# Down-projection of a hybrid block: block products, seven for eight, in two passes, with weight differences from adding transfers

## The chip, the cores and the metric

One Trainium2 chip, one core. The metric is the device time of one launch in microseconds, the median of three runs. Five engines work side by side, each with its own queue: TensorE (PE), VectorE (DVE), ScalarE (ACT), GpSimd (POOL) and SyncE (SP, which here only issues transfers).

## What is computed

One layer of a two-branch block for 640 tokens (512 latent tokens and 128 context tokens, D_MODEL = 1024, D_FF = 2816), in f32. The change touches its last stage, the down-projection of the gated ConvFFN and the residual behind it:

```python
def conv_ffn(h, w_up, w_conv, b_conv, w_down):
    u = h @ w_up                       # 640 x 1024 by 1024 x 5632
    u = conv_general_dilated(u, ...) + b_conv     # depthwise, width 3
    a, g = jnp.split(u, 2, axis=-1)
    return (a * jax.nn.silu(g)) @ w_down          # 640 x 2816 by 2816 x 1024

h2 = rmsnorm(x, g_ffn) * (1 + sc2) + sh2
x = x + gt2 * conv_ffn(h2, w_up, w_conv, b_conv, w_down)
```

## The kernel before

**Products in f32.** Every f32 operand is split into a high part (fp32r, written by ScalarE) and a low part (value less high part, a subtraction on GpSimd or VectorE). A product is three matmuls: high by high, high by low, low by high.

**Up-projection.** The 2816 gate channels are 22 tiles (NF) of 128, the first two plain, the other 20 by block products: 7 products P1 to P7 for 8, each of 4 k-tiles by 320 columns, 84 matmuls a tile. The loop over cycles c stands in each engine's program. GpSimd makes the weight sums S1 and S3 (`pooled`) and the low parts of six weight blocks (`unit_low`, L880). ScalarE makes the high parts (`unit_high`, L2199), takes P1 out (`taken`), and does the middle tap of the convolution (`first_tap`, L2172) and the SiLU (`gate_silu`, L2179). VectorE adds the products (L2976, L2983), does the outer taps (`conv_ahead` L2901, `conv_behind` L2908), the sums S2 and S4, and `gate_product` (L2922), which leaves the activations of tile j in `prod[:, j, :]`, 128 channels by 640 tokens.

**Down-projection.** w_down comes in 22 chunks: column half c (512 columns), two rows of 128 channels each. SyncE loads a chunk as two transfers of 256 KB into `wraw` (L640, two slots), ScalarE writes the high part `whi` (L2220, waits until TensorE has done with the slot), GpSimd the low part `wlo` (L713). TensorE (`token_major`, L1533 to L1535) runs, per chunk, 5 token tiles by 2 rows by 3 matmuls of 512 columns. The high parts of the activations are ScalarE's (`act_high_part`, L2227), the low parts VectorE's (`act_low_part`, L3002). The first chunk has buffers of its own (`first_raw`, `first_hi`, `first_lo`), so that it starts beside the last cycle of the up-projection. A token tile is finished by `residual` on VectorE (L2814: product by gate row; L2817: added to x), and its store is issued by ScalarE. The five stores of the first column half go out in mid-stage.

```python
for n in range(N_DOWN):
    c, q = n // 11, n % 11
    pe.wait_ge(lo_done, L_DOWN + n + 1)
    ...
    for t in range(NT) if n else (4, 0, 1, 2, 3):
        for k in range(2):
            mm = token_major(DOWN_BANK[t, c], a_hi, a_lo, 0, t, w_hi[:, k, :], w_lo[:, k, :], ...)
```

The order of all this is written out by hand: each engine runs its own list, and counters (semaphores) say what may start.

## Time and profile before

| | |
|---|---|
| median of 3 runs | 970.99 us (970.53 to 971.38) |
| span of the profiled execution | 968.6 us |
| its own time | not given apart from the span; the median is 2.4 us above the span |
| TensorE, VectorE, ScalarE, GpSimd busy | 98%, 62%, 45%, 52% |
| TensorE clock granted | full in all 40 slices |
| HBM read, written | 101.45 MB, 4.47 MB |

The span runs from the first to the last instruction of the program; a run's time holds the launch around it as well. The down-projection is the last 150 us of the span, the up-projection by block products the 240 us before it. "Busy" for TensorE is the time with a matmul in flight, and several are in flight at once: the pace, start to start, is the number to read. "Idle before, releaser" names the engine whose work ended a wait.

### The profile page before, as it was taken

To read this page: it belongs to the slowest core of one execution; us is meant where nothing else is said; L and a number is where in the kernel's file an instruction comes from. 1 tells how busy PE (TensorE), PEld (TensorE's weight loads), DVE (VectorE), ACT (ScalarE), POOL (GpSimd) and SP (SyncE) were. 2 spreads that over 40 slices of the span, in tenths; PEclk is the share of its full clock that TensorE was granted. 3 is DMA by queue.
4 is the path that set the end of the run, shared out by engine and by line. 5 is a ranking of instruction groups with operands and counts; after the bars stand their busy time and mean duration, and the time that the engine had idled before them with its cause. 6 is when DMAs were issued, how large, how long until landed. Compare 5 with 4: busy or idle time off the path is not lost.

```text
span 968.6 us, 18808 instructions
## 1 busy us (share of the span) xinstructions
PE 952.3 (98%) x7513; PEld 866.9 (89%) x7513; DVE 603.2 (62%) x1087; ACT 434.7 (45%) x683; POOL 503.9 (52%) x361
## 2 busy tenths in 40 slices
PE   6999999999999999999999999999999999999998
PEld 5799899977888899999987999999999999888886
DVE  6508359963575769434937998777777778903002
ACT  5244165523766564342404465555555556511110
POOL 1386723323332317772724378888888885433331
PEclk9999999999999999999999999999999999999999
DMA  9896222126011133888641313222222222322331
GB/s 335 270 157 97 78 76 55 58 77 185 23 30 38 45 86 100 265 251 296 236 152 44 88 45 87 88 86 84 82 83 82 83 83 72 121 81 82 105 107 55
DMA packets 127826, 108.20 MB, mean 112 GB/s; under 512 B 8342, under 2 KB 104571, under 8 KB 127483
## 3 DMA queue, kind: packets, MB, share of 16 engines
q1 hardware_dynamic: 122728, 99.81, 34.1%
q0 software_dynamic: 1696, 3.25, 2.3%
q10 hardware_dynamic: 3315, 3.94, 1.1%
q8 instruction: 60, 0.98, 0.4%
q14 instruction: 27, 0.22, 0.1%
HBM read 101.45 MB, written 4.47 MB: 109 GB/s over the span
## 4 chain that ended last, share of the span: by engine, by line
PE 87%; DVE 5%; SPq 2%; issue 2%; POOL 1%; ACT 1%; DMA 1%; DVEq 0%; POOLq 0%; ACTq 0%
PE PA L1649 6%; PE PA L1647 6%; PE PA L1648 6%; PE PJ L923 6%; PE PJ L928 5%; PE PJ L924 5%; PE PA L1533 3%; PE PA L1535 3%; PE PA L1534 3%; PE PJ L1533 3%; PE PJ L1535 3%; PE PJ L1534 3%; PE PJ L1441 2%; PE PA L1367 2%; PE PJ L1442 2%
## 5 line engine op out<-in xcount | busy, mean ns | idle before, releaser
L713 POOL TENSOR_TENSOR wlo<-wraw,whi 128x1024 fp32r<-128x1024 f32 x53 | 133.1, 2513 | 257.4 <-ACT whi L1704 167.4
L923 PE MATMUL PJ<-h_hi,whi 128*128 128x320 f32 x336 | 104.8, 320 | 0.1
L924 PE MATMUL PJ<-h_lo,whi 128*128 128x320 f32 x336 | 101.1, 309 | 0.0
L928 PE MATMUL PJ<-h_hi,wlo 128*128 128x320 f32 x336 | 76.5, 309 | 0.0
L1704 ACT ACTIVATE whi<-wraw 128x1024 fp32r<-128x1024 f32 x39 | 41.0, 1052 | 71.8 <-PE PJ L928 23.2
L923 PEld LDWEIGHTS PJ<-h_hi,whi 128*128 128x128 f32 x336 | 63.0, 188 | 5.8 <-issue 3.6
L2220 ACT ACTIVATE whi<-wraw 128x1024 fp32r<-128x1024 f32 x21 | 22.3, 1060 | 98.6 <-PE PA L1535 51.6
L924 PEld LDWEIGHTS PJ<-h_lo,whi 128*128 128x128 f32 x336 | 63.1, 188 | 0.0
L880 POOL TENSOR_TENSOR behind<-behind_val,behind 128x512 fp32r<-128x512 f32 x40 | 52.0, 1301 | 19.0 <-ACT behind L2199 19.0
L1649 PE MATMUL PA<-h_hi,behind 128*128 128x320 f32 x192 | 59.3, 309 | 0.0
L928 PEld LDWEIGHTS PJ<-h_hi,wlo 128*128 128x128 f32 x336 | 56.1, 188 | 0.0
L2901 DVE SCALAR_TENSOR_TENSOR PJ<-u_all,vec,PJ 128x641 f32<-128x641 f32 x44 | 39.0, 887 | 18.6 <-ACT PJ L2172 18.6
L1535 PE MATMUL PA<-whi,prod_lo 128*128 128x512 f32 x124 | 48.3, 389 | 0.0
L771 POOL TENSOR_TENSOR wlo<-wraw,whi 128x256 fp32r<-128x256 f32 x24 | 17.0, 737 | 57.7 <-ACT whi L1704 57.7
L2814 DVE TENSOR_TENSOR down_diag<-PJ,g_rows 128x512 f32<-128x512 f32 x4 | 2.8, 690 | 65.3 <-PE PJ L1535 65.3
L2172 ACT ACTIVATE PJ<-u_all,vec 128x641 f32<-128x641 f32 x44 | 38.9, 884 | 5.6 <-DVE prod L2923 3.4
L2199 ACT ACTIVATE behind<-behind_val 128x512 fp32r<-128x512 f32 x40 | 25.0, 625 | 34.8 <-POOL behind_val L891 34.4
L1647 PE MATMUL PA<-h_hi,behind 128*128 128x320 f32 x128 | 39.6, 310 | 0.5 <-issue 0.5
L2908 DVE SCALAR_TENSOR_TENSOR PJ<-u_all,vec,PJ 128x641 f32<-128x641 f32 x44 | 39.2, 890 | 1.5
L1647 PE MATMUL PA<-h_hi,ahead 128*128 128x320 f32 x128 | 39.7, 310 | 0.2 <-DVE u_all L2984 0.2
L1648 PE MATMUL PA<-h_lo,behind 128*128 128x320 f32 x128 | 39.6, 309 | 0.0
L1647 PE MATMUL PA<-T_hi,ahead 128*128 128x320 f32 x128 | 39.6, 309 | 0.0
(593 smaller groups left out, 3234.3 us busy)
## 6 DMA issues: line engine op xcount, KB each, us to landing
wraw<-in_w_in_dram SPq DMA_DIRECT2D x72, 256.0 KB, 3.2
ada_rest<-in_w_ada_dram SPq DMA_DIRECT2D x32, 512.0 KB, 6.1
wraw<-in_w_up_dram SPq DMA_DIRECT2D x48, 256.0 KB, 3.8
wraw<-in_w_down_dram SPq DMA_DIRECT2D x42, 256.0 KB, 3.0
raw_even<-in_w_up_dram SPq DMA_DIRECT2D x40, 256.0 KB, 3.6
ada<-in_w_ada_dram SPq DMA_DIRECT2D x16, 512.0 KB, 7.5
out_dram<-x ACTq DMA_DIRECT2D x10, 256.0 KB, 2.1
x_rows<-in_x_sample_dram SPq DMA_DIRECT2D x2, 1024.0 KB, 6.5
```

What stands on the lines that cost most here:

```text
L713: pool.tensor_tensor(wlo[:, slot, 0:k, :], wraw[:, slot, 0:k, :], whi[:, slot, 0:k, :].bitcast(F32), ALU.subtract).then_inc(lo_done, done)
L880: pool.tensor_tensor(unit_lo[name], value_of(j, name), unit_hi[name].bitcast(F32), ALU.subtract).then_inc(lo_done, 1)
L923: pe.matmul(out, whi[:, slot, w0 + k, :], hi(k)[:, tok], start=start and k == k0, stop=False)
L924: pe.matmul(out, whi[:, slot, w0 + k, :], lo(k)[:, tok], start=False, stop=False)
L928: mm = pe.matmul(out, wlo[:, slot, w0 + k, :], hi(k)[:, tok], start=False, stop=stop and k == k1 - 1)
L1533: pe.matmul(psum(*bank), act_hi_[:, k, tok], w_hi, start=start, stop=False)
L1534: pe.matmul(psum(*bank), act_hi_[:, k, tok], w_lo, start=False, stop=False)
L1535: return pe.matmul(psum(*bank), act_lo_[:, k, tok], w_hi, start=False, stop=stop)
L1647: pe.matmul(out, w_hi[:, k, :], b_hi[:, k, :], start=k == 0, stop=False)
L1648: pe.matmul(out, w_hi[:, k, :], b_lo[:, k, :], start=False, stop=False)
L1649: mm = pe.matmul(out, w_lo[:, k, :], b_hi[:, k, :], start=False, stop=k == 3)
L1704: act.activation(whi[:, slot, :, :], wraw[:, slot, :, :], ACT.Copy).then_inc(hi_done, done)
```

## The change

The 512 latent tokens' part of the down-projection is done by block products. Its operands are halved three ways: tokens (near 0 to 255, far 256 to 511), the 22 tiles of channels (k and k + 11, KH = 11), the output columns (0 to 511 and 512 to 1023). Seven products stand for eight; each is 2 token tiles by 11 steps by 3 matmuls of 512 columns. The 128 context tokens ("C") stay plain.

- **First pass**, 11 steps: P1, P2, P3 and the context tokens, 30 matmuls a step. Raw rows k and k + 11 are loaded whole (two transfers of 512 KB, `down_rows`, into `d_raw`, two slots). P3 needs a difference of activations, which VectorE forms (`third`, `second_fourth`, `first_of`).
- **Second pass**, 11 steps: P5, P7, P6, P4, 24 matmuls a step, with differences of weights. Two of the four weight blocks of a step are formed ahead, in the up-projection: SyncE loads a row (512 KB), ScalarE writes it negated (`ahead_negative`), GpSimd issues a transfer that adds other rows to it out of HBM (`accum_op`), and SyncE stores it in `ahead_dram`; eleven times, in cycles 4 to 14. The other two are made on VectorE (`weight_sums`).
- **Low parts**: half of them by transfers. ScalarE writes the high part negated, and a transfer from GpSimd's queue adds the raw value out of HBM (`landing_low`). The others are VectorE's (`weight_low`, `far_low_units`). GpSimd makes none in this stage.
- **Three sets** of high and low weights (`W_SETS`), the last three steps of the second pass run product by product (`N_LAST`), products are taken out by ScalarE between the passes (`taken_out`), GpSimd and VectorE share the final sums, and SyncE issues all stores.
- The convolution of the last channel tile goes through SBUF (`conv_of`) and stands later in the queues, since the PSUM banks go to P1.

The diff, cut to what the text speaks of:

```diff
+                q = j - FIRST_AHEAD - 2
+                if 0 <= q < KH:
+                    sp.wait_ge(ahead_sum[q % 2], AHEAD_SUM[q % 2] + 16 * (q // 2 + 1))
+                    sp.dma_start(ahead_dram[q], d_ahead[q % 3][:, :, :]).then_inc(ahead_stored[q % 3], 16)
+                q = j - FIRST_AHEAD
+                if 0 <= q < KH:
+                    if q == 0:
+                        sp.wait_ge(h2lo_set, 2 * NK + 4)
+                    elif q >= 3:
+                        sp.wait_ge(ahead_stored[q % 3], AHEAD_STORE + 16 * (q // 3))
+                    sp.dma_start(d_ahead[q % 3][:, :, :], w_dn_v[:, q, :].rearrange("p (c n) -> p c n", c=2)).then_inc(ahead_in[q % 3], 16)
...
+            def down_rows(n):
+                if n == 0:
+                    sp.wait_ge(lo_done, C_WIN + LOWS["A12", NF - 2])
+                elif n == 1:
+                    sp.wait_ge(up_ps, BLOCKS + 2 * N_PLAIN + PRODUCTS["P4", NF - 1])
+                elif n - 2 < KH:
+                    sp.wait_ge(hi_done, H_DOWN + 3 * (n - 2) + 2)
+                    sp.wait_ge(actlo_set, PART_LOW["weight", n - 2])
+                else:
+                    sp.wait_ge(actlo_set, PART_LOW["far", n - 2 - KH])
...
+                for h in range(2):
+                    rows = w_dn_v[:, n % KH + KH * h, :].rearrange("p (c n) -> p c n", c=2) if h or n < KH else ahead_dram[n - KH]
+                    sp.dma_start(d_raw[n % 2][:, 2 * h:2 * h + 2, :], rows).then_inc(raw_in[n % 2 ^ 1], 16)
...
+                q = c - FIRST_AHEAD
+                if 0 <= q < KH:
+                    pool.wait_ge(ahead_neg, 1 + q + 1)
+                    pool.dma_start(d_ahead[q % 3][:, :, :], ahead_rows(q), accum_op=ALU.add).then_inc(ahead_sum[q % 2], 16)
                 unit_low(c, "A12")
...
+            def landing_low(n):
+                k = n % KH
+                if n < KH:
+                    pool.wait_ge(hi_done, H_DOWN + 3 * n + 3)
+                    out, rows = d_far[n % W_SETS][:, :, :], w_dn_v[:, k + KH, :].rearrange("p (c n) -> p c n", c=2)
+                else:
+                    pool.wait_ge(hi_done, H_DOWN + 3 * n + 2)
+                    out, rows = d_low(n, 1), ahead_dram[k, :, 1, :]
+                pool.dma_start(out, rows, accum_op=ALU.add).then_inc(low_landed[n % W_SETS], 16)
+            for n in range(KH):
+                landing_low(n)
...
+            for n in range(KH):
+                slot, last = n % W_SETS, n == KH - 1
+                t_hi, t_lo = c_hi[slot][:, 0, :], c_lo[slot][:, 0, :]
+                s_hi4, s_lo4 = c_hi[slot][:, 1, :], c_lo[slot][:, 1, :]
+                pe.wait_ge(actlo_set, PART_LOW["rows", n])
+                if n == 0:
+                    pe.wait_ge(prod_set, NF - 1)
+                for i in range(2):
+                    mm = down(d_bank("P1", i), tile_of(a_hi[slot][:, 0, :], i), tile_of(a_lo[slot][:, 0, :], i), n, 0, n == 0, last)
+                if last:
+                    mm.then_inc(dn_done, 1)
+                pe.wait_ge(actlo_set, PART_LOW["last", n])
+                if n == 0:
+                    pe.wait_ge(add_set, ADDED["U2", NF - 1])
+                for c in range(2):
+                    mm = down(d_bank("C", c), tile_of(t_hi, 0), tile_of(t_lo, 0), n, c, n == 0, False)
+                mm.then_inc(dn_ps, 1)
+                pe.wait_ge(low_landed[n % W_SETS], landed_low(n))
+                if n == 0:
+                    pe.wait_ge(add_set, ADDED["C21", NF - 1])
+                for i in range(2):
+                    mm = down(d_bank("P2", i), tile_of(a_hi[slot][:, 1, :], i), tile_of(a_lo[slot][:, 1, :], i), n, 2, n == 0, last)
+                if last:
+                    mm.then_inc(dn_done, 1)
+                mm = down(d_bank("C", 0), tile_of(t_hi, 1), tile_of(t_lo, 1), n, 2, False, last)
+                if last:
+                    mm.then_inc(dn_done, 1)
+                pe.wait_ge(actlo_set, PART_LOW["fourth", n])
+                if n == 0:
+                    pe.wait_ge(add_set, ADDED["C11", NF - 1])
+                for i in range(2):
+                    mm = down(d_bank("P3", i), tile_of(s_hi4, i), tile_of(s_lo4, i), n, 3, n == 0, last)
+                if last:
+                    mm.then_inc(dn_done, 1)
+                mm = down(d_bank("C", 1), tile_of(t_hi, 1), tile_of(t_lo, 1), n, 3, False, last)
+                mm.then_inc(dn_ps, 1)
...
+            for k in range(KH - N_LAST):
+                for p, name in enumerate(("P5", "P7", "P6", "P4")):
+                    sum_ready(name, k)
+                    if k == 0:
+                        pe.wait_ge(ev_set, E_DOWN + {"P5": 2, "P7": 4, "P6": 7, "P4": 8}[name])
+                    for i in range(2):
+                        mm = sum_product(name, k, i)
+                    if p % 2:
+                        mm.then_inc(dn_ps, 1)
+            for name in D_LAST:
+                for i in range(2):
+                    for k in range(KH - N_LAST, KH):
+                        if i == 0:
+                            sum_ready(name, k)
+                        mm = sum_product(name, k, i)
+                    mm.then_inc(dn_done, 1)
...
+            def down_high(n, h):
+                units = slice(2 * h, 2 * h + 2)
+                if n < KH or h == 0:
+                    act.wait_ge(raw_in[n % 2 ^ 1], raw_down(n))
+                else:
+                    act.wait_ge(sum_set, T_DOWN + 2 * (n - KH) + 2)
+                if n == 0:
+                    product_done("P5", NF - 1)
+                elif n == 1:
+                    product_done("P7", NF - 1)
+                elif n == 2:
+                    product_done("P2", NF - 1)
+                else:
+                    act.wait_ge(dn_ps, 2 * (n - W_SETS) + h + 1)
+                act.activation(d_hi[n % W_SETS][:, units, :], d_raw[n % 2][:, units, :], ACT.Copy).then_inc(hi_done, 1)
+            def down_negative(n):
+                out, units = (d_far[n % W_SETS][:, :, :], slice(2, 4)) if n < KH else (d_near[n % W_SETS][:, 1:2, :], slice(1, 2))
+                act.wait_ge(hi_done, H_DOWN + 3 * n + (2 if n < KH else 1))
+                if KH <= n < KH + W_SETS:
+                    act.wait_ge(dn_ps, 2 * (n - W_SETS) + 2)
+                act.activation(out, d_hi[n % W_SETS][:, units, :].bitcast(F32), ACT.Copy, scale=-1.0).then_inc(hi_done, 1)
+            def first_half(n):
+                down_high(n, 0)
+                down_negative(n)
...
+                if m == NF - 1:
+                    act.wait_ge(lo_done, L_DOWN)
+                    down_negative(0)
+                    down_high(1, 0)
+                    fourth_high(0)
+                    down_high(1, 1)
+                    down_negative(1)
+                    early_high(0)
+                    down_rows_high(1)
+                    fourth_high(1)
+                    early_high(1)
...
+            def weight_sums(k):
+                n = KH + k
+                raw = d_raw[n % 2]
+                dve.wait_ge(raw_in[n % 2 ^ 1], raw_down(n))
+                dve.tensor_tensor(raw[:, 3, :], raw[:, 3, :], raw[:, 0, :], ALU.subtract).then_inc(sum_set, 1)
+                dve.wait_ge(sum_set, T_DOWN + 2 * k + 1)
+                dve.tensor_tensor(raw[:, 2, :], raw[:, 2, :], raw[:, 3, :], ALU.subtract).then_inc(sum_set, 1)
...
+                if c == NF - 1:
+                    third(0)
+                    weight_low(0)
+                    rows_low(0)
+                near_sum("C21", c, "P4", ug[:, near], ug[:, near])
+                if c == NF - 1:
+                    last_low(0)
+                far_sum("C12", c, "P3", tmp[:, :], ua[:, c % 2, :])
                 fourth_sum(c + 1)
                 if c == NF - 1:
-                    act_low_part(2)
-                elif c < NF:
-                    last_sum(c)
+                    second_fourth(0)
+                last_sum(c)
+                if c < NF - 1:
                     conv(c, 1)
-            for k in range(4, 10):
-                act_low_part(k)
-            for k in range(10, NF):
-                act_low_part(k)
+            fourth_low(0)
+            first_of(0)
+            third(1)
+            second_fourth(1)
+            weight_low(1)
+            rows_low(1)
+            last_low(1)
+            first_of(1)
+            fourth_low(1)
+            early_low(0)
+            conv(NF - 1, 1)
+            conv(NF - 1, 0)
+            gate_product(NF - 1)
+            for k in range(2, KH):
+                third(k)
+                early_low(k - 1)
+                second_fourth(k)
+                weight_low(k)
+                rows_low(k)
+                last_low(k)
+                first_of(k)
+                fourth_low(k)
+            early_low(KH - 1)
+            weight_sums(0)
+            weight_low(KH)
+            sums_low(0)
+            weight_sums(1)
+            far_low_units(0)
...
+            for k in range(1, KH):
+                weight_low(KH + k)
+                sums_low(k)
+                if 2 <= k < 6:
+                    context_out((k - 2) // 2, k % 2)
+                if k + 1 < KH:
+                    weight_sums(k + 1)
+                far_low_units(k)
```

Where instructions stand now, in three places. First GpSimd, in one cycle of the up-projection (cycle 5; the L numbers of the changed kernel are its own). `behind_val` is S3 or S4, `s_val` S1. Before:

```order
L880 TENSOR_TENSOR behind<-behind_val,behind 128x512
L880 TENSOR_TENSOR behind<-wraw,ahead 128x512
L880 TENSOR_TENSOR ahead<-raw_even,ahead 128x512
L891 TENSOR_TENSOR s_val<-raw_even 128x512
L880 TENSOR_TENSOR ahead<-s_val,ahead 128x512
```

With the change:

```order
L989 TENSOR_TENSOR behind<-behind_val,behind 128x512
L1006 DMA d_ahead_204<-in_w_down_dram 128x2x512
L989 TENSOR_TENSOR behind<-wraw,ahead 128x512
L989 TENSOR_TENSOR ahead<-raw_even,ahead 128x512
L1000 TENSOR_TENSOR s_val<-raw_even 128x512
L989 TENSOR_TENSOR ahead<-s_val,ahead 128x512
```

One adding transfer stands between the low part of S4 and that of A12, in eleven cycles; everything else keeps its place.

VectorE behind the last product of the convolution; before it has the low parts of the activations and the final sums:

```order
L2923 TENSOR_TENSOR prod<-PJ,cg 128x128
L3002 TENSOR_TENSOR prod_lo<-prod,act_mid 128x640 x11
L3002 TENSOR_TENSOR prod_lo<-prod,act_late 128x640 x7
L2814 TENSOR_TENSOR down_diag<-PA,g_rows 128x512
```

With the change, in the second pass, steps 0 to 2 (L3347, L3349: `weight_sums`; L3357: `weight_low`; L3340: `sums_low`; L3364: `far_low_units`; d_raw_206 and 207 are the two slots):

```order
L3347 TENSOR_TENSOR d_raw_206<-d_raw_206 128x512
L3349 TENSOR_TENSOR d_raw_206<-d_raw_206 128x512
L3364 TENSOR_TENSOR d_far_202<-d_raw_207,d_hi_196 128x1024
L3357 TENSOR_TENSOR d_near_197<-d_raw_206,d_hi_194 128x512
L3340 TENSOR_TENSOR prod_lo<-prod,s_hi_224 128x2x256
L3347 TENSOR_TENSOR d_raw_207<-d_raw_207 128x512
L3349 TENSOR_TENSOR d_raw_207<-d_raw_207 128x512
L3364 TENSOR_TENSOR d_far_200<-d_raw_206,d_hi_194 128x1024
L3357 TENSOR_TENSOR d_near_198<-d_raw_207,d_hi_195 128x512
```

Each `far_low_units` of one slot stands behind the two `weight_sums` of the other slot.

SyncE, the loads of w_down; before two slots of half chunks:

```order
L698 DMA first_raw_194<-in_w_down_dram 128x512
L640 DMA wraw<-in_w_down_dram 128x512 x8
L652 DMA g_rows<-gate_dram 128x2048
L640 DMA wraw<-in_w_down_dram 128x512 x34
```

With the change, across the border of the passes:

```order
L788 DMA d_raw_206<-in_w_down_dram 128x1024 x2
L788 DMA d_raw_207<-ahead_dram 128x1024
L788 DMA d_raw_207<-in_w_down_dram 128x1024
L788 DMA d_raw_206<-ahead_dram 128x1024
L788 DMA d_raw_206<-in_w_down_dram 128x1024
```

A load is now twice 512 KB, and in the second pass half of it comes from `ahead_dram`.

## Rows read from the trace of the kernel before

**Rows 1.** The page: span, TensorE's busy time, GB/s in 40 slices.
```profile
span 968.6 us, 18808 instructions
...
PE 952.3 (98%) x7513; PEld 866.9 (89%) x7513; DVE 603.2 (62%) x1087; ACT 434.7 (45%) x683; POOL 503.9 (52%) x361
...
GB/s 335 270 157 97 78 76 55 58 77 185 23 30 38 45 86 100 265 251 296 236 152 44 88 45 87 88 86 84 82 83 82 83 83 72 121 81 82 105 107 55
```

**Rows 2.** Timeline, ScalarE: start us, us, engine, line, operation [idle before <-releaser].
```profile
849.13 1.06 ACT L2220 ACTIVATE whi<-wraw 128x1024 fp32r<-128x1024 f32 x1 [4.48 <-PE PJ L1535]
855.93 1.06 ACT L2220 ACTIVATE whi<-wraw 128x1024 fp32r<-128x1024 f32 x1 [5.74 <-PE PJ L1535]
```

**Rows 3.** Windows: us, busy PE, PEld, DVE, ACT, POOL; clock, DMA share, GB/s.
```profile
815.00:965.00 150.00, 149.45 (x658) 123.06 (x657) 43.72 (x49) 35.29 (x41) 51.38 (x21) 1.00 0.26 88
```

**Rows 4.** Windows, the same columns, in the up-projection.
```profile
700.00:800.00 100.00, 100.00 (x684) 100.00 (x683) 77.68 (x147) 53.87 (x89) 83.97 (x65) 1.00 0.30 87
```

**Rows 5.** Timeline, GpSimd, cycles of the up-projection.
```profile
600.45 1.30 POOL L880 TENSOR_TENSOR ahead<-wraw,ahead 128x512 fp32r<-128x512 f32 x1 [0.37 <-ACT ahead L2199]
...
612.58 1.29 POOL L880 TENSOR_TENSOR ahead<-raw_even,ahead 128x512 fp32r<-128x512 f32 x1 [0.37 <-ACT ahead L2199]
...
711.00 1.29 POOL L880 TENSOR_TENSOR ahead<-raw_even,ahead 128x512 fp32r<-128x512 f32 x1 [0.38 <-ACT ahead L2199]
...
760.27 1.30 POOL L880 TENSOR_TENSOR ahead<-raw_even,ahead 128x512 fp32r<-128x512 f32 x1 [0.37 <-ACT ahead L2199]
...
800.58 1.48 POOL L880 TENSOR_TENSOR ahead<-s_val,ahead 128x512 fp32r<-128x512 f32 x1 [0.80 <-ACT ahead L2199]
```

**Rows 6.** Timeline, ScalarE, the SiLU of one cycle.
```profile
807.23 0.71 ACT L2179 ACTIVATE cg<-PJ 128x641 f32<-128x641 f32 x1 [0.48 <-DVE PJ L2908]
```

**Rows 7.** Transfers of GpSimd: issues (timeline), then KB and us to landing (page).
```profile
40.97 0.95 POOL L719 DMA_DIRECT2D kc_tok<-in_cache_na_k_dram  x1 [22.82 <-PE PA L972]
...
46.15 0.77 POOL L724 DMA_DIRECT2D vc<-in_cache_na_v_dram  x1
...
q0 software_dynamic: 1696, 3.25, 2.3%
...
kc_tok<-in_cache_na_k_dram POOLq DMA_DIRECT2D x1, 512.0 KB, 3.9
vc<-in_cache_na_v_dram POOLq DMA_DIRECT2D x1, 512.0 KB, 4.4
```

**Rows 8.** Timeline, TensorE: first matmul of the last P5; border to the down-projection.
```profile
803.69 0.31 PE L1647 MATMUL PA<-T_hi,ahead 128*128 128x320 f32 x1
...
814.10 0.31 PE L1649 MATMUL PA<-h_hi,behind 128*128 128x320 f32 x1
814.28 0.47 PE L1533 MATMUL PJ<-first_hi,act_early 128*128 128x512 f32 x1
```

**Rows 9.** Timeline, VectorE: conv_ahead of channel tile 20, and the last residual.
```profile
810.82 0.88 DVE L2901 SCALAR_TENSOR_TENSOR PJ<-u_all,vec,PJ 128x641 f32<-128x641 f32 x1
...
964.73 0.69 DVE L2814 TENSOR_TENSOR down_diag<-PA,g_rows 128x512 f32<-128x512 f32 x1
965.46 0.69 DVE L2817 TENSOR_TENSOR x<-x,down_diag 128x512 f32<-128x512 f32 x1
```

**Rows 10.** One line's instructions, L3002: duration ns min/median/max.
```profile
L3002 DVE TENSOR_TENSOR prod_lo<-prod,act_mid x12: 811/813/3031, 817.5 to 836.3; 128x640 fp32r<-128x640 f32 x12
```

**Rows 11.** A load pair of w_down: issue (timeline), landing of all 50 (L640), window.
```profile
859.49 0.80 SPq L640 DMA_DIRECT2D wraw<-in_w_down_dram  x2
...
DMA to landing us min/median/max: 2.6/3.1/7.5
...
862.00:863.00 1.00, 1.00 (x7) 0.81 (x6) 0.00 (x0) 0.27 (x1) 0.00 (x0) 1.00 0.27 102
```

**Rows 12.** DMA issues, window 815 to 965: the load of the gate rows.
```profile
g_rows<-gate_dram SPq DMA_DIRECT2D x1, 1024.0 KB, 7.6
```

**Rows 13.** Windows, the first 10 us.
```profile
0.00:10.00 10.00, 3.22 (x16) 3.25 (x17) 6.84 (x12) 3.32 (x4) 0.19 (x4) 1.00 0.80 283
```

457 lines of the change are left out of this document (319 added, 138 removed).

## Prediction, made before the changed kernel ran

> **What bounds the kernel now.** I read the page first: TensorE is busy 98% of the span [rows 1]. A busy share says little of the pace, so I took the stretch of the down-projection: one of its 22 weight chunks follows the other every 6.80 us (849.13 to 855.93), and what ScalarE waits for there is TensorE [rows 2]. A chunk has 30 matmuls, so a matmul of 512 columns takes 0.2267 us, and 660 of them 149.6 us. The stretch from 815 to 965 has 149.45 us of them [rows 3]: TensorE is the bound and has no pause. In the up-projection before it TensorE is full too, but GpSimd is 84% busy and ScalarE 54% [rows 4]. Granted clock: 1.00 in every stretch, the higher of the two levels.
>
> **Matmuls removed.** First pass, 11 steps of 30 matmuls, second pass, 11 steps of 24: 594 for 660, all of 512 columns. 66 x 0.2267 = **-15.0 us** if TensorE stays fed. The rest asks whether it does.
>
> **Up-projection, extra work in a loop that is nearly full.** Four cycles of GpSimd take 49.27 us (711.00 to 760.27), 12.32 each, and so do 84 matmuls. Early, before the cycles fall into TensorE's step, one took 12.13 (600.45 to 612.58) [rows 5]. So the round GpSimd, ScalarE, VectorE, ScalarE, GpSimd has 0.19 us to spare per cycle. Its waits, 0.37 and 0.80 of GpSimd and 0.48 of ScalarE, are for each other, none for TensorE [rows 5, 6]. The change puts one 1024-wide negation on ScalarE (1.06, of which 0.97 is pace) ahead of the SiLU, which waits 0.48 there now [rows 6], so +0.49; and one transfer issue on GpSimd (0.77 to 0.95 [rows 7], I take 0.85) ahead of a 0.36 wait, so +0.49 too, at the same time. A cycle is then 12.62 for 12.32: 11 cycles x 0.30 = 3.3 us late. P5's low part is ready at 800.58 + 1.48 = 802.06 and its matmuls start at 803.69 [rows 5, 8]: 1.6 us of reserve. **+1.7 us**. Ends: 0 (if the issue overlaps) and +6 (if an adding issue takes 1.3 us).
>
> **Start of the down-projection.** The first down matmul now starts at 814.28, at once behind the last of the up-projection [rows 8]. In the change VectorE must, from the end of conv_ahead at 811.74 (start 810.82, pace 0.92), do conv_behind, gate_product, third(0), weight_low(0) of 1024 elements and rows_low(0) of 512. By the 0.69 for 512 elements and 0.81 for 640 [rows 9, 10], 256 take about 0.42 and 1024 about 1.2; the chain ends at 815.7, **+1.5 us**. P2, the third matmul group of step 0, then wants the low part that is landed by an adding transfer. The negation for it stands on ScalarE behind first_tap(21), which waits for C21, now at 815.9 on VectorE behind those low parts; it ends at 818.0, and GpSimd issues then. Plain GpSimd transfers of 512 KB land in 3.9 and 4.4 us [rows 7]; beside 2 MB of loads (the next rows, and g_rows, which took 7.6 [rows 12]) I take 5. TensorE is free for it at 818.5: **+4.6 us**, ends +3.5 and +8. Behind that, the last channel's convolution on VectorE and ScalarE (four steps of 0.9 and a SiLU, each waiting for the other) holds VectorE until 831.0, so that rows_low(2) comes at 834.6 for 834.0: **+0.7 us**.
>
> **First pass, steady.** Per step of 6.80 us VectorE has 6 ops of 256 (0.34 each in a row), 2 of 512 and one of 1024, 4.3 us, ScalarE three of 1024, two of 512 and two of 256, about 4.6: fed, and gaining over a us a step. 1.5 MB per step over 6.8 us is 230 GB/s, under the 335 that the first slices move [rows 1]. **0**.
>
> **Second pass, the term that decides.** VectorE's order in a step k is weight_low, sums_low, weight_sums(k+1), far_low_units(k). weight_sums(k+1) needs the rows of step k+1, and SyncE issues those only when far_low_units(k-1) has freed their buffer. So far(k-1), load, weight_sums(k+1), far(k) is one closed chain: the two buffers don't overlap, since far(k) stands behind a wait for the other one's load. Its period:
> - the load. Now, SyncE issues two transfers of 256 KB from 859.49 on, and their bytes flow into the stretch 862 to 863 [rows 11]. The second is issued 0.4 later and lands 3.1 after that [rows 11], so 3.5 for 0.5 MB. The change loads 1 MB: 0.5 MB more at 335 GB/s is 1.6, so 5.1. The adding transfer of the step before, 256 KB, falls right beside it: +0.8. **5.9 us**;
> - weight_sums: 0.73 (a dependent step, 964.73 to 965.46) and 0.62 (0.69 less the overlap with what follows) [rows 9], far_low_units 1.2, and 0.05 of signalling: **2.6 us**.
>
> Together 8.5 us per step, where 24 matmuls take 5.44. Let T be the end of the first pass. sums_high(0) waits until TensorE has finished step 9 (T-6.8), so far(0) ends at T-2.8; far(1) follows at T+6.0, since sums_high(1) stands behind the last eviction. P6(2) would start at T+13.6 and far(2) comes at T+14.5: from step 2 on the chain leads. far(9) comes at T+6.0+8x8.5 = T+74.0, far(10) at T+76.4, and 66 matmuls (15.0 us) stand behind it: T+91.5. Unhindered, 264 matmuls take 59.9. **+31.6 us**.
> Ends of the load: below 4.6 (3.1 us of bytes and some 1.5 around them) without the neighbour, above 7.6 (the 1 MB of g_rows in this stretch, [rows 12]): 8 x 1.3 = 10 us less, 8 x 1.7 = 14 more.
> The Trainium skill, "DMA: Bandwidth & Descriptors", section "Anatomy of one DMA", fits a transfer issued by GpSimd as 2.0 us plus bytes over 436 GB/s. For 1 MB that would be 4.4, a chain of 7.0 and a sum 12 us below mine; the row (3.1 where the fit says 2.6 for 256 KB) speaks against the fit here, and the time still stays far above before.
>
> **Tail.** Now two VectorE steps follow the last product (964.73, 965.46), and the span ends 2.5 us behind the second [rows 1, 9]. The change ends with the same two; GpSimd's last adds fall about 1 us before the end, and may meet them: **+0.3**.
>
> **Sum.** 968.6 - 15.0 + 1.7 + 1.5 + 4.6 + 0.7 + 31.6 + 0.3 = 994.0 us of span. The runs' median, 970.99, is 2.4 above the profiled span (the profiled execution's own time isn't given apart), so **996 us** against 970.99. A measurement of this kernel tells apart about 0.2%, 2 us.
>
> **Rivals.**
> 1. *The chain doesn't bind.* If the loads of the second pass run ahead in a way that I misread, 31.6 falls to the 1.1 us of the last step's buffer wait: 965.9, faster. Against it: the period must be under 5.44, so a load under 2.9 us, and 1 MB alone takes 3.1 at 335 GB/s. For it: only a mistake of mine about who waits. Chance 0.08, with 0.02 for a time within 0.2%.
> 2. *Forecast*, 982 to 1010. Chance 0.72.
> 3. *The clock falls in the pauses.* The second pass leaves TensorE idle some 3.1 us in each step. The rows show a 6.8 us wait at the start with a granted clock of 1.00 [rows 13], and almost no pause behind it, so no row tells what a train of pauses does. At half the level a matmul takes up to 0.453: if half of a step ran so, 8.2 us still hide in 8.5; if all did, 10.9 of TensorE lead, 8 x 2.4 and 15 at the end: some 1030. The Trainium skill, "TensorE: Matmul & The Clock Gate", Part 1, says that an idle engine goes back to the lower level, which is this rival. Chance 0.08.
> 4. *Adding transfers are slow.* If one of 512 KB holds the DMA engines for over 3.7 us (6.8 less 3.1 of loads), the first pass turns to DMA: at twice that, +3.7 for some 9 steps, and the second pass's load 1.5 longer: 1040. At just under it, 1005. 3.25 MB of GpSimd's transfers took 2.3% of the span's DMA time, 22 us, or 3.4 us per 512 KB [rows 7], mostly small pieces; none adds. Chance 0.1.
>
> **Numbers.** 996, range 978 to 1016: it reaches down over the shorter load (986) with no loss in the up-projection and the shorter wait at the start (983) and some 5 for signalling that I count too high, and up over the longer load (1010), the longer wait at the start, and the mild form of 4. Faster 0.08, within 0.2% 0.02, slower 0.90.
>
> **What would show it.** Second pass: VectorE waits at weight_sums for the DMA d_raw (about 4 us a step), TensorE waits about 3 us a step for d_far, one P6 every 8.5 us, DMA share under a half. First pass: one pause of 4 to 5 us at its start behind a DMA into d_far, then 6.80 a step. Up-projection: GpSimd's period 12.6 in eleven cycles, with TensorE pausing under 2 us in all. I am wrong if the steps of the second pass follow at 5.5 us, if TensorE's clock drops, or if the first pass is slower than 6.8 a step.

## The result, and the profile after

The changed kernel takes 1017.65 us (median of four executions), the kernel before 970.76 beside it. One of the four executions, at 3218.7, was disturbed; the other three are 1014.21, 1017.28 and 1018.02, and the ratio is theirs. It is 1.047, 95% interval 1.0451 to 1.049: slower, and 1.65 us above my range (1.28 by the median of the three). The profiled execution took 1014.21 us, its span is 1012.4 where I forecast 994.0.

The page of the changed kernel: TensorE's busy time (part 1), slices (part 2), the two DMA queues that matter (part 3).

```profile
span 1012.4 us, 19085 instructions
PE 953.1 (94%) x7447; PEld 860.3 (85%) x7447; DVE 678.9 (67%) x1221; ACT 498.5 (49%) x778; POOL 500.6 (49%) x385
...
PEclk9999999999999999999999999999999989999968
DMA  9895222234110145887512257777642268965551
...
q1 hardware_dynamic: 127336, 125.50, 39.3%
q0 software_dynamic: 7856, 17.67, 11.0%
```

TensorE is no longer at 98% [rows 1], and its clock is no longer at the top in every slice. What it waits for, and how long, from 800 us on (us in total, times, longest):

```profile
PE PA L1819 <- DVE d_far L3364: 23.3, 9, 7.6
PE PA L1819 <- DMA d_far<-in_w_down_dram: 8.1, 1, 8.1
PE PA L1819 <- DMA d_near<-ahead_dram: 4.0, 4, 1.4
PE PJ L1819 <- DVE a_lo L3317: 1.3, 1, 1.3
```

Before, TensorE had almost no pause from 815 to 965 [rows 3]. Four places carry the difference; the bold figures are what each adds to the span, in us.

**Up-projection.** GpSimd's timeline of one cycle; the second s_val is one cycle behind the first:

```profile
692.09 1.73 POOL L1000 TENSOR_TENSOR s_val<-raw_even 128x512 f32<-128x512 f32 x1
...
701.71 1.20 POOL L1006 DMA_DIRECT2D d_ahead<-in_w_down_dram  x1
702.49 1.76 POOL L989 TENSOR_TENSOR behind<-raw_even,ahead 128x512 fp32r<-128x512 f32 x1
703.75 1.75 POOL L989 TENSOR_TENSOR ahead<-wraw,ahead 128x512 fp32r<-128x512 f32 x1
705.01 1.74 POOL L1000 TENSOR_TENSOR s_val<-wraw 128x512 f32<-128x512 f32 x1
```

A cycle is 12.92 (692.09 to 705.01) for 12.32 [rows 5]. The issue costs 0.78 until the next operation starts, and the three operations behind it show 1.75 for 1.30 at an unchanged spacing, a lag of 0.45 that is paid at the next wait: 1.23 together. Against it stand the 0.37 wait that was there and is used up, and some 0.2 of a stretched operation behind s_val (1.29 where it was 1.47 before). The last matmul of the up-projection starts at 819.33, before at 814.10 [rows 8]: **+5.2**.

**Start of the down-projection.** TensorE's first down matmul and P2 of step 0, and GpSimd's issue for it:

```profile
820.97 0.50 PE L1819 MATMUL PJ<-d_hi,a_hi 128*128 128x512 f32 x1 [1.33 <-DVE a_lo L3317]
832.12 0.80 PE L1819 MATMUL PA<-d_hi,a_hi 128*128 128x512 f32 x1 [8.14 <-DMA d_far<-in_w_down_dram]
```

```profile
823.52 0.90 POOL L1025 DMA_DIRECT2D d_far<-in_w_down_dram  x1 [8.21 <-ACT d_far L2454]
```

From issue to TensorE it is 8.6 us. The windows (busy PE, PEld, DVE, ACT, POOL; granted clock, DMA share, GB/s) show what ran beside it, and that the clock fell to half, the lower of its two levels:

```profile
825.00:830.00 5.00, 0.00 (x0) 0.00 (x0) 4.93 (x11) 3.76 (x7) 0.86 (x1) 0.73 0.96 261
830.00:835.00 5.00, 2.88 (x7) 2.31 (x8) 3.11 (x4) 3.27 (x4) 0.00 (x0) 0.50 1.05 275
835.00:840.00 5.00, 5.00 (x18) 3.95 (x17) 4.86 (x11) 2.60 (x5) 0.86 (x1) 0.75 0.54 122
...
985.00:990.00 5.00, 4.31 (x9) 2.97 (x10) 2.97 (x4) 0.57 (x1) 0.47 (x2) 0.50 0.35 56
990.00:995.00 5.00, 5.00 (x21) 4.08 (x20) 1.48 (x3) 0.00 (x0) 4.84 (x4) 0.89 0.00 0
```

The last matmul of the first pass ends at 906.87, 85.9 us behind the first; 330 x 0.2267 are 74.8. So **+11.1**: 8.1 of waiting, and 3.0 behind it, nearly all at the lower clock (twelve matmuls from 832.12 to 837.40, 0.43 us apart instead of 0.23, make 2.6).

**Second pass.** The chain that ended last, in order of time (start, us, what):

```profile
948.90 6.10 DMA d_raw<-in_w_down_dram
955.02 0.70 DVE d_raw L3347
955.75 0.69 DVE d_raw L3349
956.44 1.15 DVE d_far L3364
957.97 6.10 DMA d_raw<-in_w_down_dram
```

It is the closed chain of the forecast, four links with nothing of TensorE in it, 9.07 us a round here (948.90 to 957.97), 9.04 over the eight rounds of far_low_units from 911.40 to 983.73. The pass lasts from 906.87 to 1004.18, 97.3 us for 59.9: **+37.4**.

**Tail.** VectorE's timeline at the end, then GpSimd's:

```profile
995.53 1.77 DVE L3488 TENSOR_TENSOR d_raw<-d_raw,g_rows 128x512 f32<-128x512 f32 x1
...
1004.13 3.05 DVE L3499 TENSOR_TENSOR x<-x,d_raw 128x512 f32<-128x512 f32 x2
1007.10 0.68 DVE L3501 TENSOR_TENSOR down_diag<-PJ,g_rows 128x512 f32<-128x512 f32 x1
...
1009.14 0.69 DVE L3505 TENSOR_TENSOR x<-x,down_diag 128x512 f32<-128x512 f32 x1
```

```profile
1003.68 2.94 POOL L1064 TENSOR_TENSOR x<-x,d_raw 128x512 f32<-128x512 f32 x2 [1.83 <-DVE d_raw L3494]
```

The span ends 8.2 us behind TensorE; before it was 4.1: **+4.1**. Two smaller terms belong to the sum: -15.0 for the matmuls that went, and +1.5 by which the first down matmul stands further behind the last of the up-projection (1.64 for 0.18). That is +44.3. The spans differ by 43.8; the 0.5 is, up to rounding, that the 660 matmuls of before ran 150.25 us (814.28 to 964.53), not 149.6.

### The profile page after: what moved, and what is told of

It is laid out like the page before. It is cut to its first block, busy times and chain, and to the rows that moved or that the text cites. A ratio compares the mean times of both kernels' runs of the same rounds, so it can differ in the third digit from the quotient of the medians.

```text
span 1012.4 us, 19085 instructions
## 1 busy us (share of the span) xinstructions
PE 953.1 (94%) x7447; PEld 860.3 (85%) x7447; DVE 678.9 (67%) x1221; ACT 498.5 (49%) x778; POOL 500.6 (49%) x385
## 4 chain that ended last, share of the span: by engine, by line
PE 63%; POOL 14%; DVE 7%; DMA 6%; issue 5%; SPq 2%; ACT 2%; ACTq 0%; POOLq 0%; DVEq 0%
POOL behind L989 6%; PE PJ L1077 6%; PE PJ L1082 5%; PE PJ L1078 5%; DMA d_raw<-in_w_down_dram 5%; PE PA L1801 2%; PE PA L1802 2%; PE PA L1803 2%; POOL s_val L1000 2%; POOL ahead L989 2%; PE PJ L1595 2%; PE PA L1521 2%; PE PJ L1600 2%; PE PJ L1596 2%; POOL behind_val L1000 1%
## 5 line engine op out<-in xcount | busy, mean ns | idle before, releaser
L822 POOL TENSOR_TENSOR wlo<-wraw,whi 128x1024 fp32r<-128x1024 f32 x32 | 80.6, 2521 | 166.5 <-ACT whi L1926 166.2
L1926 ACT ACTIVATE whi<-wraw 128x1024 fp32r<-128x1024 f32 x39 | 41.0, 1052 | 71.0 <-PE PJ L1082 22.8
L2446 ACT ACTIVATE d_hi<-d_raw 128x1024 fp32r<-128x1024 f32 x44 | 45.7, 1050 | 52.6 <-DMA d_raw<-in_w_down_dram 48.3
L3185 DVE SCALAR_TENSOR_TENSOR PJ<-u_all,vec,PJ 128x641 f32<-128x641 f32 x42 | 37.2, 885 | 17.5 <-ACT PJ L2394 17.5
L1025 POOL DMA_DIRECT2D d_near<-ahead_dram x11 | 9.5, 868 | 77.7 <-ACT d_near L2454 77.7
L1801 PE MATMUL PA<-T_hi,ahead 128*128 128x320 f32 x128 | 40.2, 314 | 2.6 <-POOL ahead L989 2.5
L1025 POOL DMA_DIRECT2D d_far<-in_w_down_dram x11 | 9.5, 864 | 65.2 <-ACT d_far L2454 65.2
L2421 ACT ACTIVATE ahead<-s_val 128x512 fp32r<-128x512 f32 x20 | 12.7, 633 | 56.5 <-POOL s_val L1000 53.7
L1803 PE MATMUL PA<-T_hi,ahead 128*128 128x320 f32 x128 | 39.6, 309 | 0.0
```

The source lines that it names most:

```text
L822: pool.tensor_tensor(wlo[:, slot, 0:k, :], wraw[:, slot, 0:k, :], whi[:, slot, 0:k, :].bitcast(F32), ALU.subtract).then_inc(lo_done, done)
L1801: pe.matmul(out, w_hi[:, k, :], b_hi[:, k, :], start=k == 0, stop=False)
L1803: mm = pe.matmul(out, w_lo[:, k, :], b_hi[:, k, :], start=False, stop=k == 3)
L1926: act.activation(whi[:, slot, :, :], wraw[:, slot, :, :], ACT.Copy).then_inc(hi_done, done)
L2421: act.activation(unit_hi[name], value_of(j, name), ACT.Copy).then_inc(hi_done, 1)
L2446: act.activation(d_hi[n % W_SETS][:, units, :], d_raw[n % 2][:, units, :], ACT.Copy).then_inc(hi_done, 1)
```

## The experiments

Each run is a variant of the changed kernel (1017.65 us, ratio 1.047) unless it says otherwise. Ratios are to the kernel before, run on the same chip beside it. All in one table:

| Run | us, median | ratio, 95% interval |
|---|---|---|
| e1: order of the second pass | 990.41 | 1.0204 (1.0187 to 1.0221) |
| e2: step 0's far low part by GpSimd | 1013.68 | 1.0446 (1.0428 to 1.0465) |
| e3: negation and issue moved | 1010.37 | 1.0407 (1.039 to 1.0425) |
| e4: plain landings | 1007.9 (one) | |
| e5: GpSimd's last additions narrowed | 1015.07 (one) | |
| e6: second pass, near part by GpSimd | 1013.26 | 1.0442 (1.0424 to 1.0459) |
| e7: all low parts by GpSimd | 1016.07 | 1.0475 (1.0458 to 1.0493) |
| e8: e7 with e1 and e3 | 984.47 | 1.0147 (1.013 to 1.0164) |
| e9: second pass, near part by VectorE | 1007.66 | 1.0383 (1.0366 to 1.0401) |
| e10: e1, e2, e3, e9 | 978.73 | 1.008 (1.0063 to 1.0097) |
| e11: e10, VectorE in the first pass too | 976.49 | 1.0059 (1.0042 to 1.0076) |
| e12: e11, two last steps by product, convolution spread | 970.59 | 0.9996 (0.9984 to 1.0008) |
| e13: e2, convolution spread | 1010.8 | 1.0412 (1.0397 to 1.0428) |
| e14: e11, two last steps by product | 975.96 | 1.0059 (1.0039 to 1.0079) |
| e15: e12, last additions by VectorE | 967.29 | 0.9971 (0.9961 to 0.9981) |

### e1: is it the chain?

```diff
+            far_low_units(0)
             weight_sums(1)
-            far_low_units(0)
...
+                far_low_units(k)
                 if k + 1 < KH:
                     weight_sums(k + 1)
-                far_low_units(k)
```

> VectorE's order in the second pass is changed alone: far_low_units(k) comes ahead of weight_sums(k+1). Nothing is left out. Theory (the closed chain far_low(k-1), load, weight_sums(k+1), far_low(k), 9.07 us a step): the load of step k+2 now has a whole step more, and a round over two steps is load 6.5 + sums 1.4 + high part 1.0 + low part 1.2 = 10.1 us, 5.05 a step, under the 5.44 of 24 matmuls. The second pass takes 60 to 68 us instead of 97.7, VectorE waits for the DMA d_raw under 1 us a step, and TensorE's clock stays at 1.00 there: about 982 us, 26 to 37 less than the changed kernel's 1014 to 1018. Rival A (the transfers' total, not their order, bounds the second pass): 1.25 MB a step at what the slices show now gives no faster step, under 5 us gained. Rival B (the clock is low there for another reason than the pauses): some 15 us gained and a granted clock under 0.9 in 900 to 970.

Measured: 27.2 us less, by the change of order alone. The second pass lasts 73 us. Its waits and two windows:

```profile
PE PA L1819 <- DVE d_far L3364: 8.7, 2, 5.1
PE PA L1819 <- DMA d_far<-in_w_down_dram: 8.4, 1, 8.4
```

```profile
906.00:938.00 32.00, 31.43 (x138) 25.37 (x137) 28.20 (x30) 18.89 (x25) 10.35 (x11) 1.00 0.69 189
938.00:970.00 32.00, 22.87 (x89) 17.60 (x88) 19.96 (x25) 12.77 (x17) 8.77 (x9) 0.84 0.71 195
```

Until 938 TensorE is fed; the wait for d_far falls from 23.3 in nine to 8.7 in two, and these two are the last steps'. The closed chain is shown to be the cause of 24 of the 37.4 us of this pass. The pass is not at the 60 to 68 expected: far_low_units now follow each other every 5.9 us on average (909.74 to 956.62, eight steps), and the last ones come late, since a load that took 5.3 us took 7.9 the next time (issued 940.84 and 945.46, used 946.17 and 953.41). From 930 to 960 the DMA engines are 0.88 busy; that loads and adding transfers get into each other's way there is the likely reason, and e10, which has no adding transfer in this pass, supports it. The clock wasn't at 1.00 to the end either: it was 0.84 from 938 to 970.

### e2 and e13: the first wait

```diff
-            for n in range(KH):
+            pool.wait_ge(lo_done, L_DOWN)
+            pool.wait_ge(hi_done, H_DOWN + 2)
+            pool.tensor_tensor(d_far[0][:, :, :], d_raw[0][:, 2:4, :], d_hi[0][:, 2:4, :].bitcast(F32), ALU.subtract).then_inc(lo_done, 1)
+            for n in range(1, KH):
                 landing_low(n)
```

> Step 0 of the first pass alone: its two far low parts are formed by one subtraction of GpSimd (1024 elements wide) instead of a negation and an adding transfer; the other 21 steps are as in the changed kernel. Nothing is left out. Theory (TensorE waits 8.1 us for the landing of the first adding transfer, and the clock falls to 0.50 behind that wait): the high part is there at 816.9, GpSimd takes some 2.6, so P2(0) starts without a wait; 8.1 us go, and the clock's some 3 us with them: 10 to 11 us less, first pass from 821 on at 6.8 a step and clock 1.00 from 825 to 840. Rival: the next steps' adding transfers are as late, so that the wait only moves to step 1 or 2: under 3 us gained, a wait of 5 us or more for DMA d_far in step 1.

Measured: the wait of 8.1 is gone, and yet only 4.0 us of the median, with overlapping intervals. In the trace TensorE now waits later, at the rows of step 2, and in steps 3 and 5 for landings:

```profile
839.44 0.60 PE L1824 MATMUL PJ<-d_hi,a_hi 128*128 128x512 f32 x1 [2.34 <-DVE a_lo L3324]
...
851.74 0.50 PE L1824 MATMUL PA<-d_hi,a_hi 128*128 128x512 f32 x1 [0.90 <-DMA d_far<-in_w_down_dram]
```

VectorE reaches step 2 at 835.83, because the last channel's convolution holds it, as in the changed kernel, where TensorE was late itself. far_low_units(0) comes 2.5 us earlier (900.43 for 902.93), so no more is left of 8.1. Three things took the rest: the later waits (2.3, 0.9 and 0.5 us); the clock, with eight matmuls 0.43 us apart from 822.61 on and eight more from 839.44 on, 1.6 us each; and a first matmul at 821.59 for 820.97. So the 10 to 11 us expected didn't come. The rival was right that the wait only moves, but named a landing in step 1 or 2, where it is VectorE in step 2. e13 spreads the convolution besides (on ScalarE too, whose calls aren't shown):

```diff
-            conv(NF - 1, 1)
-            conv(NF - 1, 0)
-            gate_product(NF - 1)
             for k in range(2, KH):
...
                 fourth_low(k)
+                if k == 2:
+                    conv(NF - 1, 1)
+                elif k == 4:
+                    conv(NF - 1, 0)
+                elif k == 5:
+                    gate_product(NF - 1)
```

> The changed kernel with two edits in the first pass: step 0's far low parts by GpSimd (as in the second run), and the last channel's convolution spread over steps 2 to 5 of VectorE and ScalarE. Nothing is left out; the second pass is as in the changed kernel. Theory (the 8.1 us wait for the first landing lay beside a lateness of VectorE: with the wait gone, the last channel's convolution ahead of step 2 held VectorE until 836 and took the gain back; both have to go): the first pass runs from 821 without a pause, T comes 8 to 11 us earlier than in the changed kernel, and the whole 8 to 11 us less, 1003 to 1008. Rival (what took the gain back is the adding transfers' pace or the second pass's loads): 1012 or more, TensorE waiting for d_far in steps 1 to 4.

Measured: 6.9 us less than the changed kernel, 2.9 less than e2, and 2.8 above the 1003 to 1008 expected. far_low_units(0) comes at 896.04, 6.9 earlier. The wait for a_lo of step 2 is gone; 2.3 us for landings in steps 1 and 2 and 1.8 at the first matmul are left. So two latenesses lay side by side: taking away the one that was seen in the waits brought the second pass 2.5 us forward, taking away the other as well brought 4.4 more.

### e3: the up-projection

```diff
+                ahead_negative(m - FIRST_AHEAD)
                 unit_high(m + 1, "S1", "P5")
...
-                ahead_negative(m - FIRST_AHEAD + 1)
...
                 pooled(c + 1, "S3", "A11", "A21", ALU.subtract)
+                q = c - FIRST_AHEAD
+                if 0 <= q < KH:
+                    pool.wait_ge(ahead_neg, 1 + q + 1)
+                    pool.dma_start(d_ahead[q % 3][:, :, :], ahead_rows(q), accum_op=ALU.add).then_inc(ahead_sum[q % 2], 16)
                 unit_low(c + 1, "S3")
```

> In the up-projection alone, ScalarE's negation stands ahead of the high part of S1 (where it waits 3.2 us for GpSimd) and GpSimd's issue of the adding transfer stands behind the sum S3 (where it waits 0.80 for ScalarE). Nothing is left out. Theory (the issue takes some 1.2 us of GpSimd, of which 0.37 lie in a wait now; the cycle is 12.93 instead of 12.32): the issue lies in the 0.80 wait, cycle 12.3 to 12.7, and the last up matmul comes 3 to 5 us earlier than 819.33; the whole 3 to 5 us faster than the changed kernel. Rival A (the issue slows GpSimd wherever it stands, by what it still does behind): cycle stays 12.8 to 12.9, under 1 us. Rival B (ScalarE's negation is what makes the cycle long): cycle 12.32 at once, with the same gain, but ScalarE's waits, not GpSimd's, are what changes in the trace.

```profile
699.87 1.30 POOL L1000 TENSOR_TENSOR s_val<-wraw 128x512 f32<-128x512 f32 x1
...
704.64 1.20 POOL L1011 DMA_DIRECT2D d_ahead<-in_w_down_dram  x1
...
712.19 1.30 POOL L1000 TENSOR_TENSOR s_val<-raw_even 128x512 f32<-128x512 f32 x1
```

Measured: a cycle of 12.32, that of before, and the first down matmul at 815.69 for 820.97: 5.3 us earlier; the whole 7.3 us less. The issue is still 1.20 long: it costs nothing where it lies in a wait. Both moves were made at once, so this run doesn't tell ScalarE's share apart. The changed kernel's trace puts the limit on GpSimd: its wait for ScalarE ahead of `ahead` is gone, while ScalarE waits 3.16 us for GpSimd's s_val in the same cycle (693.90).

### e4: what adding costs a transfer

```diff
-                pool.dma_start(out, rows, accum_op=ALU.add).then_inc(low_landed[n % W_SETS], 16)
+                pool.dma_start(out, rows).then_inc(low_landed[n % W_SETS], 16)
```

> All 22 landing transfers of GpSimd in the down-projection (both passes) are plain copies instead of adding ones, with the same sizes, places and waits. Left out with it: the subtraction of the high part from these far low parts, so they hold the weights themselves. Theory (an adding transfer takes 1.8 times the DMA time of a plain one per byte and lands later): first landing 5 to 6 us instead of 8.3 (TensorE's first wait 3 us shorter), DMA share in 840 to 900 about 0.70 to 0.75 instead of 0.85 to 1.0, second pass's load 6.5 to 6.0: 5 to 10 us less. Rival (the landing is late because of the loads beside it, whatever it does with the bytes): DMA share and first wait as before, within 2 us of the changed kernel's profile.

What is left out is the subtraction of the high part. The DMA queues and issues from 830 to 900 (packets, MB, share of 16 engines; count, KB each, median us to landing), first of the changed kernel, then of this one:

```profile
q1 hardware_dynamic: 2880, 10.49, 44.8%
q0 software_dynamic: 1640, 5.67, 44.7%
...
d_raw<-in_w_down_dram SPq DMA_DIRECT2D x16, 512.0 KB, 5.4
d_far<-in_w_down_dram POOLq DMA_DIRECT2D x9, 512.0 KB, 8.4
```

```profile
q1 hardware_dynamic: 2864, 10.42, 42.0%
q0 software_dynamic: 1485, 5.13, 21.8%
...
d_raw<-in_w_down_dram SPq DMA_DIRECT2D x16, 512.0 KB, 4.2
d_far<-in_w_down_dram POOLq DMA_DIRECT2D x9, 512.0 KB, 5.6
```

Per MB an adding transfer holds the DMA engines 7.9% of the 70 us against 4.25% of a plain one, 1.85 times as long. It lands 2.8 us later and makes the loads beside it land 1.2 later. So the theory holds for the transfer itself, and this one execution, 1007.9, is 6.3 us below the profiled one of the changed kernel, where 5 to 10 were expected. For the first landing it holds only by half: from issue to use it takes 6.8 us (823.42 to 830.26) where 5 to 6 were expected and the adding one took 8.6, so adding makes 1.8 us of it, and the first wait is still 6.4. In the second pass a load with a plain neighbour takes 5.9 us on average for 6.5, and far_low_units follow every 8.4 us for 9.04.

### e5 and e15: the tail

```diff
-                x_ = x2[:, i, BANK:D]
-                pool.tensor_tensor(x_, x_, d_raw[1][:, 2 + i, :], ALU.add).then_inc(pooled_set, 1)
+                x_ = x2[:, i, BANK:BANK + 1]
+                pool.tensor_tensor(x_, x_, d_raw[1][:, 2 + i, 0:1], ALU.add).then_inc(pooled_set, 1)
```

The other two of the four additions are cut in the same way.

> The last four additions of GpSimd into x2 (two 512-wide columns' worth for e0, two for q) are made on one column each; left out with it: the other 511 columns of these four additions. Their waits and counts stay. Theory (at the end VectorE and GpSimd slow each other: VectorE's 0.69 us operations take 1.77, and its two last-but-one additions take 3.05 together, held behind GpSimd's): VectorE's operations are 0.69 again and the tail behind TensorE's last matmul is 4.2 to 5 us instead of 8.1, the profile 3 to 4 us shorter than the changed kernel's. Rival (the tail is long because VectorE has more to do in it or waits for products): tail as before, within 1 us.

```profile
1006.67 1.27 DVE L3499 TENSOR_TENSOR x<-x,d_raw 128x512 f32<-128x512 f32 x2
...
1009.91 0.69 DVE L3505 TENSOR_TENSOR x<-x,down_diag 128x512 f32<-128x512 f32 x1
```

Measured: the pair that took 3.05 takes 1.27, and the span ends 4.7 us behind TensorE's last matmul (1008.57) instead of 8.2. The whole was no shorter (1015.07), since this execution had lost some 4 us in the passes before; the tail is read by itself. So GpSimd's additions make the tail long. Which operations they hit can be read from the changed kernel, VectorE first, then GpSimd:

```profile
997.22 0.68 DVE L3485 TENSOR_TENSOR d_raw<-prod,PA 128x512 f32<-128x512 f32 x1
```

```profile
996.83 1.62 POOL L1055 TENSOR_TENSOR x<-x,prod 128x512 f32<-128x512 f32 x1
```

The operation with one input in PSUM (PA) keeps its 0.68 us beside GpSimd; the one with both inputs in SBUF took 1.77 (995.53, shown with the tail above; GpSimd was at work from 995.13 on). The Trainium skill, "SBUF — State Buffer", section "Who interferes with whom", says that a VectorE instruction with two inputs in SBUF contends with a GpSimd instruction that reads SBUF, and one with at most one SBUF input does not; this trace agrees in both. e15 is a use of it, on top of e12: VectorE makes the four additions itself.

> The kernel with both edits (970.59), and the last four additions of GpSimd done by VectorE; nothing left out. Theory (the two engines' operations stretch each other: 1.77 and 1.71 for 0.69): VectorE has four operations more, 2.4 us, and loses some 5 to 6 us of stretching, so the tail of 12.7 us falls to 8.5 to 10 and the whole by 3 to 4 us, to 966 to 968, faster than the kernel before. Rival (VectorE is simply the bound there, and what GpSimd takes off it is worth more than the stretching): same or longer, 970 to 973.

Measured: 967.29 for 970.59. The tail is 12.1 us (951.8 to 963.9) for 12.7 (954.6 to 967.3), not the 8.5 to 10 expected: VectorE is the bound there and has 2.4 us more to do, and takes about 3 less for being stretched, so the rival has the larger part. The rest of this execution's lead stands ahead of the last matmul, which comes 2.8 us earlier; 1.6 of that is a shorter wait for d_far in the last step (2.4 to 0.8), and 1.6 the clock: behind that wait eight matmuls of e12 were 0.43 us apart (942.65 to 946.05), and none are here. The edit, which stands behind both, doesn't explain them. The total came out as expected, 966 to 968, but not for the reason given. That the version is faster is shown; how its 3.3 us divide stays open.

### e6, e7, e9: who should form the low parts

```diff
+def by_gp(n):
+    return n >= N_DOWN // 2
...
+                if by_gp(n):
...
+                    out, units = (d_far[n % W_SETS][:, :, :], slice(2, 4)) if n < KH else (d_near[n % W_SETS][:, 1:2, :], slice(1, 2))
+                    pool.tensor_tensor(out, d_raw[n % 2][:, units, :], d_hi[n % W_SETS][:, units, :].bitcast(F32), ALU.subtract).then_inc(lo_done, 1)
+                    return
```

> In the second pass alone, GpSimd subtracts the high part of ahead's second half itself (512 wide, some 1.3 us) where the changed kernel has ScalarE's negation and an adding transfer of 256 KB. Nothing is left out; the order of VectorE stays. Theory (the adding transfer beside the load costs the closed chain some 0.8 us a step, and TensorE waits 4.0 us in all for its landings): period 8.2 to 8.4 instead of 9.07, 7 to 9 us less in all. Rival A (GpSimd's subtraction falls on weight_sums and far_low_units and stretches them as its merged additions stretched VectorE's 0.68 to 2.30): period 9 or more, no gain or a loss. Rival B (1 MB takes 6.5 us whatever runs beside it): period 9.07, within 2 us.

```profile
937.70 2.30 DVE L3391 TENSOR_TENSOR d_far<-d_raw,d_hi 128x1024 fp32r<-128x1024 f32 x1
...
945.50 0.69 DVE L3374 TENSOR_TENSOR d_raw<-d_raw 128x512 f32<-128x512 f32 x1 [2.59 <-DMA d_raw<-in_w_down_dram]
```

Measured: 4.4 us less by the medians, with intervals that overlap, and a period of 8.9 on average (911.48 to 982.56 in eight) for 9.04, not the 8.2 to 8.4 expected. Both mechanisms are there and nearly cancel: the load, from issue to use, takes 5.2 on average (4.6 to 6.1 in the eight steps) for 6.5, and far_low_units 2.30 for 1.22, since GpSimd's subtraction starts just then (937.57). The 4.0 us of waits for d_near are gone, but TensorE waits 27.6 us for d_far instead of 23.3, so nothing is gained in the profiled execution (1012.6 for 1012.4). With GpSimd in the first pass too:

> As the run before, and in the first pass too: GpSimd subtracts the far low parts itself (1024 wide, some 2.6 us a step) instead of the negations and adding transfers of 512 KB. No adding transfer is left in the down-projection. Nothing is left out. Theory (the adding transfers cost the first pass its first wait of 8.1 us and a DMA share of 0.85 to 1.0, and nothing else there): the wait and the clock's dip go, and as in the run with GpSimd in step 0 alone VectorE's last channel gives back most of it; DMA share 840 to 900 falls to some 0.45; steps of 6.8 us; 2 to 6 us less than the run before. Rival (VectorE, with 4.3 us of operations a step, is stretched by GpSimd's 2.6 us): its step grows to over 6.8 us, TensorE waits for a_lo or d_far in each step and the first pass takes 5 us or more longer.

Measured: 2.8 us more than e6, the rival in a mild form. VectorE is busy 29.7 of 30 us from 840 to 870 and TensorE waits 8.3 us for a_lo (6.5 at the longest). e8 has all of it with the better order:

> All together: GpSimd subtracts in both passes, far_low_units ahead of weight_sums in the second pass, and the moved negation and issue of the up-projection. Nothing is left out. If the costs found add up (27 for the order, 5 for the up-projection, 8 for the adding transfers of the second pass, some for the first; the DMA share of 0.88 that remained behind the order falls with the adding transfers): 966 to 978, near the kernel before. If VectorE is stretched by GpSimd: 985 or more, with VectorE busy over 90% in both passes and TensorE waiting for it.

Measured 984.47; VectorE is busy 29.4 of 30 us from 900 to 930, its own operations, stretched by GpSimd's, take 6.3 us a step (far_low_units from 898.19 to 929.85 in five), over TensorE's 5.44. So forming the parts by GpSimd is no way out. e9 gives the near part to VectorE:

```diff
-                units = slice(0, 2) if n < KH else slice(0, 1)
+                units = slice(0, 2) if n < KH or by_vec(n) else slice(0, 1)
```

`by_vec(n)` is true for all steps of the second pass.

> In the second pass alone, VectorE subtracts the high part of ahead's second half together with the first half, in one operation 1024 wide (1.2 us instead of 0.69); no adding transfer, no negation and no subtraction of GpSimd there. Nothing is left out; far_low_units stays behind weight_sums. Theory (the run with GpSimd in the second pass gained 1.0 us a step in the load, 5.5 for 6.5, and lost it again in far_low_units, stretched from 1.22 to 2.30): now only the gain stays, period 5.5 + 2.6 = 8.1, 8 to 9 us less than the changed kernel. Rival (VectorE's stretched operation was not on the chain and the load got no shorter): period 9.1, no gain.

Measured: 10.0 us less than the changed kernel (by the ratios 0.87%, 8.4 us). far_low_units follow every 8.0 us (912.96 to 977.07 in eight) where 8.1 was expected, and a load takes 5.3 on average. The adding transfer thus cost the chain 1.0 us a step (1.2 in the load), and the wider operation of VectorE, which is off the chain, cost nothing that shows.

### e10, e11, e12, e14: put together

e10 is e1 to e3 with e9; e11 has VectorE form the far low parts of steps 1 to 10 as well; e14 adds N_LAST = 2, e12 that and the spread convolution.

> Second pass as in the run before, with far_low_units ahead of weight_sums; step 0 by GpSimd; first pass otherwise with its adding transfers; moved negation and issue in the up-projection. Nothing is left out. Theory (behind the order, the second pass is held by transfers that share the DMA engines, 0.88 busy): with 0.25 MB less a step it follows at TensorE's 5.44, TensorE waits some 1 to 3 us for the last steps' d_far, clock 1.00: 970 to 978. Rival (another wait decides, VectorE's two-step round): steps of 6 us or more, 984 or more.

> As the run before, and in the first pass VectorE forms the far low parts of steps 1 to 10 itself (1024 wide, 1.2 us), GpSimd that of step 0: no adding transfer is left in the down-projection. Nothing is left out. VectorE then has 4.3 + 1.1 = 5.4 us of a 6.8 us step, so if nothing stretches it the first pass stays at 6.8 and DMA share falls to 0.45; it catches up more slowly behind the last channel's convolution, so some 1 to 3 us more waits for a_lo there than in the run before. 970 to 978, within 3 us of the run before. If the adding transfers also cost the loads of the first pass something that TensorE feels, this one is faster.

> The kernel of the run before with two further edits, nothing left out. (a) N_LAST is 2 for 3: the second pass goes step by step up to step 8, and only the last two are ordered by product. Far_low_units(10) can only be written when step 7 has freed its slot; TensorE now has step 8 to do meanwhile. (b) The last channel's convolution, whose product is wanted first in step 10, stands spread over steps 2 to 5 on VectorE and ScalarE instead of ahead of step 2. Theory (TensorE's pauses of 5.1 us at step 2 and 7.0 us for d_far at the end each also cost some 2 to 3 us of lower clock): both go, the tail grows by 2 to 4 us because the last products come closer together; 960 to 968, faster than the kernel before. Rival (the waits are only moved: VectorE is as late in steps 3 to 6, and the last two steps wait for d_far anyway): 972 or more.

> The kernel with VectorE's low parts throughout, moved order and moved issue (976.49), with N_LAST 2 for 3 alone, nothing left out. Theory (TensorE's waits of 2.4 and 4.6 us for d_far and the lower clock behind them come from the slot that step 7 frees): the waits fall to some 2.4 us, TensorE ends 5 to 7 us earlier, the tail grows by some 4: 1 to 3 us less, 973 to 976; the rest of the 5.9 us that both edits gave together came from the convolution. Rival (the last steps' waits and the tail cancel wholly): same or slower than 976.49.

Measured: e10 978.73, just above the 970 to 978 expected: from 900 to 930 TensorE is busy 30.0 of 30, so the second pass does follow at its pace with the DMA engines at 0.41, but the last steps' waits for d_far are 7.7 us where 1 to 3 were expected. e11 976.49, 2.2 less, with intervals that overlap. e14 975.96: the waits for d_far fall from 7.0 to 2.3 and TensorE ends 7.4 us earlier, but the tail behind it is 5.1 longer, and the medians differ by 0.5, which isn't clear of the noise. e12 970.59, 2.6 above the 960 to 968 expected, which had allowed 2 to 4 for the longer tail (it grew by 4.5). 5.4 of its 5.9 us came with the convolution: TensorE's wait of 5.1 for a_lo is gone, and with it a granted clock of 0.66 from 830 to 840 (1.00 now). e15's page and waits:

```profile
span 963.9 us, 19059 instructions
...
PE 937.8 (97%) x7447; PEld 854.2 (89%) x7447; DVE 690.5 (72%) x1235; ACT 480.9 (50%) x756; POOL 482.5 (50%) x360
```

```profile
PE PJ L1832 <- DVE a_lo L3345: 1.5, 2, 1.3
PE PA L1832 <- DVE d_far L3400: 0.8, 1, 0.8
```

At 0.9971 of the kernel before (interval 0.9961 to 0.9981) it is the fastest version here. Against the span of before: the down matmuls take 134.7 us for 150.25 (-15.6), the first one starts at 815.33 for 814.28 (+1.0), pauses and what the clock took are 1.8, and the tail is 12.1 for 4.1 (+8.0). That is -4.8, and the spans differ by 4.7. So the 15 us are saved after all, and half of them are spent in the tail.

## Why the prediction was wrong

The direction and the mechanism of the largest term stood; the sizes of four terms did not. 18.4 us are missing of the span (3.5, 5.8, 5.8 and 3.8 below, less the 0.5 of before). The step that failed in three of them is the price of an adding transfer: its issue (1.23 for my 0.85), its landing (8.6 for my 5) and what it costs a load beside it (1.2 for my 0.8). In two of them the clock came on top, whose drop was one of my own signs of being wrong; the fourth is GpSimd's additions in the tail. Term by term:

- **Up-projection, +1.7 forecast, +5.2 measured.** The way was right, the size of GpSimd's issue wasn't: I took 0.85 from plain issues [rows 7], and an adding one ahead of busy operations costs 1.23. The bound of +6 that I had named for 1.3 us held. e3 shows that its place made it cost.
- **First down matmul, +1.5 forecast, +1.5 measured.**
- **Start of the first pass, +4.6 and +0.7 forecast, +11.1 measured.** The failed step is "I take 5" for the landing: it was 8.6 from issue to use. Of the 3.6 that are missing, adding makes 1.8 (e4: 6.8 for the plain one). The other 1.8 the plain transfer has too; the 2 MB of loads beside it are the likely reason, which no run takes away. The clock, which I had at 1.00 here, added most of 3.0. The wait at step 2 didn't appear, being covered; e2 and e13 show it was there below.
- **First pass, steady, 0 forecast.** Right: 134 matmuls in 30 us, 1.00, at a DMA share of 0.86 to 0.97. Rival 4 asked whether an adding transfer of 512 KB holds the DMA engines for over 3.7 us; by e4's window of the changed kernel (44.7% of 70 us for 5.67 MB) it holds them 2.9.
- **Second pass, +31.6 forecast, +37.4 measured.** The head was right to 0.3 us: far(1) ended at T+5.75 for T+6.0. The failed step is "+0.8" for the neighbour. The period was 9.04 for 8.5, which with the 0.25 of the head makes 4.1 us in eight steps, all of it in the load: 6.5 for 5.9, where the sums and far_low_units took 2.56 for 2.6. Without a neighbour the load took 5.2 (e6) and 5.3 (e9), near my 5.1; with a plain one 5.9 (e4), which is my sum; with an adding one 6.5, so the neighbour cost 1.2 in the load and 1.0 in the period. Then 66 matmuls took 16.8 us for 15.0, because the clock was at 0.50 behind the last wait of 7.6. The Trainium skill's fit for transfers issued by GpSimd, "DMA: Bandwidth & Descriptors", section "Anatomy of one DMA", would make it 4.4, as an estimate; these loads are SyncE's, and the averages of the runs are 5.2 and more.
- **Tail, +0.3 forecast, +4.1 measured.** I wrote that GpSimd's additions "may meet" VectorE's steps and gave it 0.3. They did: e5 takes 3.5 of it away.
- **Rival 3 (the clock)** came in small: about 3 us behind the first wait, 1.9 at the end. The pauses of 0.9 and 2.2 us in a step until 939 left it at 1.00, which is against my rival as I had put it. From 939.92 and from 967.29 on, eight matmuls each were 0.43 us apart, 1.6 us each time; the chain, which leads there, hid them. I should have put its small form, one long wait and what follows it, into the range.

Offset and noise: with 2.4 us above the span, 1012.4 would give 1014.8, and the profiled execution had 1014.21, inside my range; the median was 3 higher, and no profile shows those 3. That the miss of the range is small says little: four terms were too small, all the same way.

## What to carry to other kernels

When two buffers are reused, write down the round from "freed" to "freed" and look at what stands in an engine's order between them: here one pair of calls in the wrong order cost 27 us, where the change could save 15. A transfer that computes is not free: price its DMA time, its landing and its issue by itself before building a loop on it, and compare it with one wider operation on the engine that already touches the data. When a wait is removed, look which other work was as late and hidden behind it.

## What the runs showed of the hardware that I had not expected

- An adding transfer from HBM into SBUF holds the DMA engines 1.85 times as long per byte as a plain one of the same queue, and lands 8.4 us after its issue where the plain one took 5.6 (e4, medians from 830 to 900).
- GpSimd's issue of it cost 1.2 us ahead of running work, 0.45 of which shows only as longer operations behind it, but 0.86 to 0.90 where GpSimd was idle; a plain one took 0.53 to 0.63 there (e4).
- Behind single waits of 8.1, 7.6 and (e11) 5.1 us the granted clock fell to 0.50 to 0.57 in a stretch of 5 us, and matmuls came every 0.43 us instead of 0.23, which cost 1.8 to 2.6 us each time. The same pause doesn't always do it: behind one of 2.2 us eight matmuls were slow in the changed kernel (939.92) and none at 930.52.
- VectorE's 0.69 us operations with two inputs in SBUF took 1.77 when GpSimd worked on SBUF beside them; one with an input in PSUM stayed at 0.68 beside it (997.22).
